# Attention heads in pairs on the two halves of the matrix array, y products inside the mixer attention, and one product for the forget sums

## What is computed

```python
def _dense_attention(q, k, v, scale):          # 8 heads, q and k 96 wide, v 64 wide
    sc = jnp.einsum('bhqd,bhkd->bhqk', q_blk, k) * scale
    p = jax.nn.softmax(sc, axis=-1)
    return jnp.einsum('bhqk,bhkd->bhqd', p, v)
...
y_a = o_a.reshape(b, s, MLA_WIDTH) * jax.nn.silu(gate_a)
```

```python
u, q, k, v, f, g_a, g_b = jnp.split(h @ w_in, cuts, axis=-1)
y_ssm = s5_ssm(u, ...)                          # a linear recurrence, 32 groups of 16 channels
z_val, z_gate = jnp.split(jax.nn.gelu(y_ssm) @ glu_w, 2, axis=-1)
y_a = z_val * jax.nn.sigmoid(z_gate)
attn = forgetting_attention(q, k, v, f + forget_b)
y_b = attn @ attn_w_out
merged = jax.nn.sigmoid(g_a) * y_a + jax.nn.sigmoid(g_b) * y_b
return merged @ w_out
```

## Time and profile before

| | us |
|---|---|
| median of 3 runs | 3795.54 |
| lowest and highest | 3791.35, 3800.80 |
| the profiled execution's own time | 3789.88 |
| its span, first to last instruction | 3788.1 |
| granted clock, mean | 0.939 |
| PE busy in the span | 3485.8 (92%) |

### The profile page before, as it was taken

The page is one execution under the profiler, slowest core; times in us unless marked ns, Lnnn a source line. Parts: engine busy times, 40 slices in busy tenths (PEclk is TensorE's granted clock), DMA queues, the critical chain, the costliest instruction groups (busy, mean ns, idle before and its releaser), DMA issues. The chain is left out here.

```text
span 3788.1 us, 43633 instructions
## 1 busy us (share of the span) xinstructions
PE 3485.8 (92%) x15562; PEld 2640.4 (70%) x15562; DVE 2004.3 (53%) x2714; ACT 1162.8 (31%) x1770; POOL 1343.3 (35%) x565
## 2 busy tenths in 40 slices
PE   7999896999996999998999999969998989999997
PEld 6646674655774788777667788758887765777886
DVE  4866684766585443595344643144437824544422
ACT  2344312344322223331333222322233303332222
POOL 3302232311231545443034344534463411434453
PEclk8999997999997999997799999979999969999998
DMA  4503463423372332354113232233234532323321
GB/s 117 176 23 119 120 209 83 131 77 109 100 233 55 105 94 83 90 96 96 45 56 117 78 96 83 71 92 96 85 92 95 95 60 55 99 69 102 98 81 64
DMA packets 586119, 363.86 MB, mean 96 GB/s; under 512 B 57810, under 2 KB 535388, under 8 KB 585692
## 3 DMA queue, kind: packets, MB, share of 16 engines
q1 hardware_dynamic: 585636, 361.51, 34.6%
q10 hardware_dynamic: 312, 0.12, 0.0%
HBM read 346.63 MB, written 12.58 MB: 95 GB/s over the span
## 5 line engine op out<-in xcount | busy, mean ns | idle before, releaser
L136 POOL TENSOR_TENSOR w_lo<-w_raw,w_hi 128x1024 fp32r<-128x1024 f32 (+2 forms) x552 | 1335.4, 2425 | 2395.5 <-ACT w_hi L128 2340.8
L142 PE MATMUL bank<-xh,w_lo 128*128 128x512 f32 x2432 | 987.5, 406 | 89.5 <-DVE xl L2108 36.5
L143 PE MATMUL bank<-xl,w_hi 128*128 128x512 f32 x2432 | 970.5, 399 | 0.0
L144 PE MATMUL bank<-xh,w_hi 128*128 128x512 f32 x2432 | 968.7, 398 | 0.0
L128 ACT ACTIVATE w_hi<-w_raw 128x1024 fp32r<-128x1024 f32 (+2 forms) x552 | 565.7, 1028 | 795.8 <-PE bank L144 728.1
L142 PEld LDWEIGHTS bank<-xh,w_lo 128*128 128x128 f32 x2432 | 468.3, 193 | 214.1 <-issue 58.2
L143 PEld LDWEIGHTS bank<-xl,w_hi 128*128 128x128 f32 x2432 | 469.1, 193 | 102.7 <-issue 4.3
L144 PEld LDWEIGHTS bank<-xh,w_hi 128*128 128x128 f32 x2432 | 467.3, 192 | 103.4
L144 PE MATMUL bank<-HH,w_hi 128*128 128x512 f32 x704 | 278.5, 396 | 0.0
L142 PE MATMUL bank<-HH,w_lo 128*128 128x512 f32 x704 | 278.5, 396 | 0.0
L143 PE MATMUL bank<-HL,w_hi 128*128 128x512 f32 x704 | 278.4, 396 | 0.0
(11 more groups left out here) (478 smaller groups left out, 4658.6 us busy)
## 6 DMA issues: line engine op xcount, KB each, us to landing
w_raw<-in_ffn_w_in_dram SPq DMA_DIRECT2D x176, 512.0 KB, 3.8
m_raw<-in_mod_w_dram SPq DMA_DIRECT2D x144, 512.0 KB, 4.8
w_raw<-in_w_in_dram SPq DMA_DIRECT2D x80, 512.0 KB, 4.0
w_raw<-in_mix_w_in_dram SPq DMA_DIRECT2D x64, 512.0 KB, 8.3
w_raw<-in_ffn_w_out_dram SPq DMA_DIRECT2D x64, 384.0 KB, 3.4
w_raw<-in_ffn_w_out_dram SPq DMA_DIRECT2D x64, 320.0 KB, 3.2
w_raw<-in_w_out_dram SPq DMA_DIRECT2D x16, 512.0 KB, 4.5
w_raw<-in_glu_w_dram SPq DMA_DIRECT2D x32, 256.0 KB, 3.0
```

Source lines behind the costliest of these rows:

```text
L136: nc.gpsimd.tensor_tensor(ring.lo[s][:, 0:width], ring.raw[s][:, 0:width], ring.hi[s][:, 0:width].bitcast(F32), ALU.subtract).then_inc(rin ...
L142: nc.tensor.matmul(out, wl, xh, start=start, stop=False)
L143: nc.tensor.matmul(out, wh, xl, start=False, stop=False)
L144: return nc.tensor.matmul(out, wh, xh, start=False, stop=stop)
```

## The change

1. The first attention runs by pairs of heads: step j is pair p, query tile q, side j % 2. `attend_a` works for one query tile of both heads: products of 128 queries, alternately into output partitions 0 to 63 and 64 to 127. `gate_pair` takes both heads at once.
2. The mixer attention runs by pair-steps g (pair, query tile). `scores(g)` issues the QT x KT products of both heads one after the other, which stand on different 64 rows, into two banks. The forget sums come from one tile `cum_hl` with the high sums in rows 0 to 7 and the low ones in rows 32 to 39 (and again from row 64 on), in one product for each head. For that the f product has 128 columns (weights repeated by `fwide`, made on DVE ahead of the powers), and the forget bias comes as a row of `vrow`, by a fourth DMA of ACT.
3. The four y chunks move from ahead of the attention into pair-steps 0 to 3, in place of gate work; ten gates instead of eight stand ahead of the attention, the other six in halves in pair-steps 4 to 15; gate 3 moves ahead of the transposes of T1. On SP the 32 DMAs to Mt stand in two halves, the first ahead of gate_out(4). gelu moves from step 2 to step 16. ACT makes w_hi of gates 0 to 2 ahead of its copies of v.

Core of the diff:

```diff
-        if j % TT == 0:
-            hold(("o", j // TT), 5 + j // TT % 2)
+        if j % (2 * TT) == 0:
+            hold(("o", j // (2 * TT)), 5 + j // (2 * TT) % 2)
...
+    def place(j):
+
+        p, q = divmod(j // 2, TT)
+        return p, q, j % 2, 2 * p + j % 2
...
-        def attend_a(h, k):
-
-            out = free(pe, ("o", h)) if k == 0 else held(("o", h))
-            r = slice(h % 2 * VH, h % 2 * VH + VH)
-            wait_read(pe, ("t", h * TT + TT - 1))
-            if h == 0:
+        def attend_a(i, keys):
+
+            p, q = divmod(i, TT)
+            out = free(pe, ("o", p)) if q == 0 and 0 in keys else held(("o", p))
+            for j in (2 * i, 2 * i + 1):
+                wait_read(pe, ("t", j))
+            if i == 0:
                 wait_read(pe, ("va", TT - 1))
-            ins = nc.tensor.matmul(out[r, :], VA[:, k, h * VH:(h + 1) * VH], PTr[h % 2][:, k, :],
-                                   start=k == 0, stop=k == TT - 1)
-            if k == TT - 1:
-                ins.then_inc(s_att, 1)
+            c = slice(q * P, (q + 1) * P)
+            for k in keys:
+                for side in range(2):
+                    h, r = 2 * p + side, slice(side * VH, side * VH + VH)
+                    ins = nc.tensor.matmul(out[r, c], VA[:, k, h * VH:(h + 1) * VH], PTr[side][:, k, c],
+                                           start=k == 0, stop=k == TT - 1)
+                    if k == q == TT - 1:
+                        ins.then_inc(s_att, 1)
...
-            if j >= TT:
-                attend_a(j // TT - 1, j % TT)
+            if j >= 2:
+                attend_a(j // 2 - 1, (0, 1) if j % 2 == 0 else (2, 3))
...
-        for k in range(TT):
-            attend_a(HA - 1, k)
+        attend_a(NA // 2 - 1, range(TT))
...
-            if q == 0 and h >= 2:
-                act.wait_ge(s_att, h - 1)
-            keep_turned(("t", j), j, PTr[h % 2][:, :, q * P:(q + 1) * P])
+            p, q, side, h = place(j)
+            keep_turned(("t", j), j, PTr[side][:, :, q * P:(q + 1) * P])
...
+        def gate_pair(p):
+
+            dve.wait_ge(s_att, 2 * p + 2)
+            read(V.scalar_tensor_tensor(SG[:, p, :], held(("o", p))[:, :], 0.5, SG[:, p, :],
+                                        ALU.mult, ALU.mult), ("o", p))
...
-        gate_head(HA - 2)
         negmax_d(1)
-        gate_head(HA - 1)
+        gate_pair(HA // 2 - 1)
...
+    fwide = mem("fwide", [P, KT, P], F32, over="VT")
+    fwh, fwl = mem("fwh", [P, KT, P], F32R, over="Kn"), mem("fwl", [P, KT, P], F32R, over="VT", skip=4 * KT * P)
...
-    cum_h, cum_l = mem("cum_h", [HF, T], F32R, over="fl0"), mem("cum_l", [HF, T], F32R, over="fl1")
+    cum_hl = mem("cum_hl", [P, T], F32R, over="fl0")
...
+    NFA = 10
...
+    for f in range(4, NFA):
+        hold(("g", f), f % 4)
+    NI = HF * TT
+    NS = NI // 2
     for i in range(4):
-        hold(("y", i), 4 + i)
-    NI = HF * TT
+        hold(("y", i), 7)
+    for f in range(NFA, NF):
+        hold(("g", f), 7)
     for j in range(NI):
-        hold(("s", j), j % 3)
-        hold(("t", j), 3 + j % 2)
-        if j % TT == 0:
-            hold(("o", j // TT), 5 + j // TT % 2)
-            hold(("g", 8 + j // TT), 7)
+        hold(("s", j), j % 4)
+        hold(("t", j), 4 + j % 2)
+    for p in range(HF // 2):
+        hold(("o", p), 6)
...
+        def taps(first, end):
+            for t in range(first, end):
+                for a in range(4):
+                    to = Mt[t * SG:(t + 1) * SG, :, 0:(CH - t) * SG].rearrange("p (q j h) c -> p q j h c", q=2, h=2)[:, a % 2, :, a // 2, :]
+                    sp.dma_start(to, Kn[32 * a:32 * a + SG, :, t * SG:P]).then_inc(s["m_in"], 16)
+
         for f in range(8):
             gate(f)
-        for f in range(5):
+        for f in range(4):
             gate_out(f)
             gate(8 + f)
         sp.wait_ge(s["m_cleared"], 1)
         sp.wait_ge(s["skip_added"], 4)
-        for t in range(CH):
-            for a in range(4):
-                to = Mt[t * SG:(t + 1) * SG, :, 0:(CH - t) * SG].rearrange("p (q j h) c -> p q j h c", q=2, h=2)[:, a % 2, :, a // 2, :]
-                sp.dma_start(to, Kn[32 * a:32 * a + SG, :, t * SG:P]).then_inc(s["m_in"], 16)
+        taps(0, CH // 2)
+        gate_out(4)
+        gate(12)
+        taps(CH // 2, CH)
         for f in range(5, 8):
             gate_out(f)
             gate(8 + f)
-        for i in range(4):
-            wait_read(sp, ("y", i))
+        for f in range(8, 10):
+            gate_out(f)
+            merge_block(f - 8)
+        wait_read(sp, ("y", 3))
...
-        quads(4, B_G + 4)
-        split_lo(nc, pool, ring, B_G + 4, 0, BLK)
-        split_lo(nc, pool, ring, B_G + 5, 1, BLK)
+        quads(4, B_G + 8)
...
+        gate(3)
...
-        for f in range(4, 8):
+        for f in range(4, NFA):
             gate(f)
-
-        pe.wait_ge(s["m_in"], 16 * 32)
-        pe.wait_ge(s["states"], 4)
-        for i in range(4):
...
+        def scores(g):
+            p, q = divmod(g, TT)
+            n = (q + 1) * P
+            out = [free(pe, ("s", 2 * g + side))[:, 0:n] for side in range(2)]
+            for side in range(2):
+                r = slice(side * 64, side * 64 + 64)
+                nc.tensor.matmul(out[side], QT[r, p, q * P:n], KTr[r, p, 0:n], start=True, stop=False)
+            for side in range(2):
+                h, r = 2 * p + side, slice(side * 64, side * 64 + H2)
+                nc.tensor.matmul(out[side], pick[r, h:h + 1].broadcast_to([H2, P]), cum_hl[r, 0:n], start=False, stop=False)
+            for side in range(2):
+                nc.tensor.matmul(out[side][:, q * P:n], ident_r[:, :], mask_r[:, :], start=False, stop=True).then_inc(s["scores"], 1)
+
+        def y_product(i):
+            if i == 0:
+                pe.wait_ge(s["m_in"], 16 * 32)
+                pe.wait_ge(s["states"], 4)
...
+        def attend(g):
+            p, q = divmod(g, TT)
+            out = free(pe, ("o", p)) if q == 0 else held(("o", p))
+            c = slice(q * P, (q + 1) * P)
+            for side in range(2):
+                wait_read(pe, ("t", 2 * g + side))
+            for k in range(q + 1):
+                for side in range(2):
+                    h, r = 2 * p + side, slice(side * 64, side * 64 + 64)
+                    ins = nc.tensor.matmul(out[r, c], VT[:, k, h * 64:(h + 1) * 64], PTr[side][:, k, :],
+                                           start=k == 0, stop=k == q)
+                    if k == q == TT - 1:
+                        ins.then_inc(s["attended"], 1)
+
+        scores(0)
+        scores(1)
+        for g in range(NS):
+            turn_probs(2 * g)
+            turn_probs(2 * g + 1)
+            if g + 2 < NS:
+                scores(g + 2)
+            if g < 4:
+                y_product(g)
+            else:
+                gate(NFA + (g - 4) // 2, (g - 4) % 2)
+            attend(g)
...
+        act.dma_start(vrow[V_FB:V_FB + 1, :].rearrange("a (x h) -> a x h", h=HF),
+                      forget_b[bass.ds(l, 1)][:, None, :].broadcast_to([1, P // HF, HF])).then_inc(s["vectors_in"], 16)
...
+        for t in range(3):
+            hi(B_G + t)
         for t in range(4):
             act.wait_ge(ring.used, B_V + 4)
             read(nc.scalar.activation(VT[:, t, :], held(("v", t)), ACT.Copy), ("v", t))
-            hi(B_G + t)
+            if t == 0:
+                hi(B_G + 3)
...
+        for j in range(4):
+            exps(j)
+        act.wait_ge(s["m_in"], 16 * 32)
...
+            if side:
+                g = j // 2
+                for i in (2 * g + 4, 2 * g + 5):
+                    if i < NI:
+                        exps(i)
+                if q == 0 and p:
+                    keep_pair(p - 1)
+                if g < 4:
+                    take_chunk(g)
+                if g >= 4 and g % 2:
+                    gate(NFA + (g - 4) // 2)
...
+        step.done(dve, V.memset(fwide[:, :, :], 0.0))
+        for i in range(0, P, 32):
+            step.done(dve, V.tensor_copy(fwide[:, :, i:i + HF], fw[:, :, :]))
+        split_dve(nc, dve, step, fwh[:, :, :], fwl[:, :, :], fwide[:, :, :]).then_inc(s["f_split"], 1)
...
+        step.done(dve, V.tensor_copy(cum_hl[:, :], cum[:, :]))
+        for r in (slice(32, H2), slice(96, 64 + H2)):
+            step.done(dve, V.tensor_tensor(cum_hl[r, :], cum[r, :], cum_hl[r, :].bitcast(F32), SUB))
```

More of the change, by code:

```diff
@@ L1037, in _ @@
             V.tensor_scalar(PX[j % 4][:, :], PX[j % 4][:, :], rinv[:, 0, j:j + 1], None, ALU.mult).then_inc(s_p, 1)
-            if q == 1 and h >= 2:
-                gate_head(h - 2)
+            if j >= 2 * TT and j % (2 * TT) == TT - 1:
+                gate_pair(j // (2 * TT) - 1)
         def negmax_d(j):
@@ L1500, in _ @@
         sp.dma_start(ych[:, :, :, :].rearrange("p t s c -> p t (s c)"), y_dram.rearrange("(t p) c -> p t c", p=P)).then_inc(s["y_in"], 16)
-        for f in range(8, 12):
+        for f in range(10, 12):
             gate_out(f)
@@ L1682, in gate @@
```

(52 more changed lines are left out.)

141 lines of the change are left out of this document (51 added, 90 removed).

## The result

The changed kernel takes 3736.2 us (median of four, 3727.7 to 3742.6) beside 3793.4 for the kernel before (3791.2 to 3800.8): 0.985 of its time, interval 0.983 to 0.986. That is 57 us less; the forecast of 3701 would have been 92 to 95 less. The profiled execution of the changed kernel is a long one, 3742.6, with a span of 3740.8.

The account below looks back on a forecast made before the run. PE was taken as the bound, busy 92% of the span. Mixer -59, first attention -25, clock at y -12 and entry +1.2 sum to -94.8, giving 3701 us; forecast band 3675 to 3735, range 3640 to 3765.

Parts of the forecast that it names:

- the second rival: Mixer attention: DVE, ACT and the gates' chain bound it, 20 us a layer more, about 3740; chance 0.10.
- First attention: First attention: column halves overlap, period 2.07 us for 2.49, earlier tail; -12.5 us a layer, -25 in all.
- Mixer attention by pairs: Mixer attention: scores, forget sums and attends of two heads side by side, 8.6 us a pair, -34.5 us for four.
- What comes instead of the wait: Ahead of mixer attention: the gates' tanh and DMA chain delays its start, +5.2 us first layer, +1.6 second.
- Clock between the y products: Mixer pair-steps with y chunks: dense pieces between them lift the clock partly, 6 us a layer, -12 in all.
- The first rival: y products run at 2.4 GHz, 28 us a layer beyond the forecast, 3645 us; chance 0.17.
- DVE's waits: Mixer pair-steps 8 to 12: gelu makes PE wait for DVE, +10 us a layer, between 0 and +20.
- Small parts: Before the injection: gate 0's 5.77 us wait goes, DVE adds 4 to 5, net 0; block entry +1.2 both layers.
- The entry: Path into the block: a fourth DMA issue of ACT, about 0.6 us with its turn, +1.2 for both layers.

Follow-up runs that it names:

- e1: The kernel before with only the first attention by pairs of heads, mixer untouched: 3769.0 us, ratio 0.994.
- e8: The changed kernel, but each step of the first attention issues the four attend products of one head only: 3756.1 us, ratio 0.990.
- e6: The changed kernel, but both attentions' attends take all key tiles of one head, then of the other: 3736.8 us, ratio 0.984.
- e9: e5 with y chunks made in pairs, so that products of 64 rows on different row halves stand side by side: 3647.1 us, ratio 0.961.
- e7: The changed kernel, but the mixer's QT x KT, forget sums and mask come head by head: 3784.6 us, ratio 0.998.
- e3: The changed kernel, but gates 8 and 9 use other banks and their tanh comes after the first turned copies: 3709.6 us, ratio 0.978.
- e2: The changed kernel, but the four y chunks stand ahead of the mixer attention again, directly behind gate 9: 3701.6 us, ratio 0.977.
- e4: As e2, but matmuls of gates 9 to 12 stand between the y groups, and gates 13 to 15 stay in the attention: 3704.8 us, ratio 0.975.
- e5: As e2, but a gelu tile starts every four steps instead of every two, over pair-steps 8 to 15: 3690.0 us, ratio 0.972.

## Why the prediction was right in sign and too large

The faster kernel was forecast and came, but the number it came with is not the forecast's: 3736 lies just above the band given with 3701 (3675 to 3735) and close to the 3740 of the second rival, which had a chance of 0.10. That rival put 20 us a layer more on DVE, ACT and the gates' chain. The mixer did take some 20 us a layer more than the sum (18 and 21), and the chain is about half of it, though ahead of the attention and not in it.

**First attention: right.** -12.5 us a layer forecast, 12.2 by the medians of e1 (8 to 15 by its interval), 11.3 in the first layer of the trace. The period of 2.07 was 2.08, the slack of DVE and ACT held. The reason, overlap of the column halves, stands since e8; that the products have to alternate, which the text took for granted, does not (e6). The Trainium skill (TensorEngine Tiling (Array Packing), Key Properties) says that different tiles can load weights and multiply in parallel; e8 and e9 agree, with 0.58 for 1.02 us, and with 1.05 for 2.08 for the four products of 64 rows in two y groups.

**Mixer attention by pairs: right.** Scores and attends side by side were to save 34.5 us a layer at full clock. Taking only the scores apart cost 22 us a layer (e7), more than its share at full clock (about 4.1 x 4 = 17), likely because a quarter of them run at 1.2 GHz. By the distances between starts at full clock, QT x KT, forget sums and attends of a pair take 6.3 us in the changed kernel and took 15.3: 9.0 less, where the prediction has 8.6. Its own terms (5.8 - 2.9, 4.0 - 1.2, 5.4 - 2.7) add up to 8.4, not 8.6, so -33.6 a layer, a slip of 0.9. The two row halves were also the lever of e9.

**What comes instead of the wait: mis-sized, one of two large errors.** "+5.2" for the first layer, with 5 us of idle; the trace has 14.39 and 12.97, and e3 shows what the wait cost, 31 us in the two layers. The mechanism was the one named, the gates' tanh chain through `stg`. What was too small was its link: I took 4.8 us for every gate from one row of before. After the change the tanhs stand at:

```profile
1746.69 0.60 ACT L1975 ACTIVATE stg<-bank 128x512 f32<-128x512 f32 x1 [10.58 <-DMA g_scratch<-stg]
1751.62 0.60 ACT L1975 ACTIVATE stg<-bank 128x512 f32<-128x512 f32 x1 [3.38 <-DMA g_scratch<-stg]
1759.93 0.60 ACT L1975 ACTIVATE stg<-bank 128x512 f32<-128x512 f32 x1 [6.77 <-DMA g_scratch<-stg]
1766.60 0.60 ACT L1975 ACTIVATE stg<-bank 128x512 f32<-128x512 f32 x1 [5.12 <-DMA g_scratch<-stg]
```

Links of 4.9, 8.3 and 6.7 us, together 5.5 us more than three of 4.8; the next 2 us come of a first tanh that starts later than in the sum and of the last tanh itself. The copy before the long link is issued at 1752.24, and stg is free again at 1759.9, 7.7 us later, where the one before took 4.3. The DMA share from 1752.6 to 1767.3 is 0.61. That the longer time comes of several transfers at once, the gate's copy beside the weights that the released gates call for, is an argument from the share; no run took it apart.

**Clock between the y products: the sign was right, half came.** "-12 in all", 6 us a layer, for dense pieces lifting the clock; the trace has 3 us at 2.4 GHz in one chunk of each layer, which is worth 3. The first rival, y at full clock (0.17), is refuted by the change's own trace (0.52) and by e2; that other work between the products can hold the clock up for a time, e4's second layer shows. The rule of the Trainium skill that stood beside it (TensorE: Matmul & The Clock Gate, Part 1) does not hold here in the form in which I gave it, that sustained activity releases the clock: in e2 the clock falls with PE without a pause. The move itself was therefore a loss: it shortened little and took away the cover of the tanh chain. e2 against the change, -39 us, is the price; 31 of it come back by the banks alone (e3).

**DVE's waits: the right size, without the clock.** "+10 a layer": in the first layer PE waits 1.45 + 4.03 + 3.19 + 1.32 = 10.0 us for DVE from pair-step 8 on. What I left out, a term put at nothing, is that the clock falls at the two long ones: it is at 1.2 GHz for 6.8 us each time, 13.7 us a layer, of which PE works some 12, so some 6 us are lost, and the window of pair-steps 4 to 15 has 0.89. From the first scores to zg the sum gives 1931 - 1777.6 less the clock's 6, 147 us; it took 157.1. The 10 us are these 6 and the 3 that did not come between the y products.

**Small parts.** The injection started as forecast, 0.8 us later after the block's first transpose than before: DVE comes later than I thought (PE waits 8.26 us for Ci, where it waited for nothing there), but for it the 5.77 us ahead of gate 0 shrink to 0.69, and the 3.59 us at T1i to 0.47 there and 1.60 ahead of the injection. The entry cost 1.5 us a layer (21.01 of idle for 19.52) for 0.6.

By the traces the start was 8 and 11 us later after the injection than in the sum, and the stretch to zg 10 us longer in each layer, together 39 us. The medians leave 38 to explain, 95 less 57. The two profiled executions lie only 47 us apart, since that of before is a quick one and that of the change a long one; the 8 us that are open there lie in the first attentions (22 us at the end of the first block instead of 25) and in the ways to the two injections.

## To carry to other kernels

Products with 64 rows or 64 columns ran two at a time here where the other half's product came next or two places on (e6, e9), and did not with scores and transposes between (e8) or with a mask of all rows between (e7); look for all such products, not only for the attention's (e9 won 43 us over e5). Before work is moved, ask what it was hiding: the y products, moved into the attention, uncovered a chain that ran on ACT and DMA. And read the granted clock itself: PE's busy share does not tell it (in e2's y stage PE is busy for 48.20 of 48.20 us, at 0.55).

## What the runs showed of the hardware

- PE can be busy without a gap and still be at 1.2 GHz: with float32 products of 64 columns, each with weights of its own, directly behind full-speed matmuls, the clock fell 5.0 us after the first of them (e2, first layer), and it stayed low for the other 43 us of the stage. With three 512-column matmuls between the groups it fell after 2.7 us in the first layer of one execution, and in the second layer of the same execution it stayed up for 41.5 us (e4).
- Column halves overlap without strict alternation: two products of one half, then two of the other, take 0.60 us where alternation takes 0.58 (e6); with scores and transposes between them 1.02 for the same eight records (e8).
- Row halves overlap with their weight loads: in e9 two products of 64 rows by 64 columns with 128 weight columns take 0.49 to 0.56 us at 1.2 GHz, what one takes alone in e2 (0.48 to 0.56), and four weight loads take 0.51 to 0.55 us, as two do in e2 (0.50 to 0.54).
